# Loads, row products and stores in another order, and a batched routing over 54 pair sums, in a two-layer hybrid trunk

## The chip, the cores and the metric

The kernel runs on 1 core of one Trainium2 chip. The metric is the device time of a run in microseconds. Engines are named as in the profile: PE (TensorE matmul), PEld (its weight loads), DVE (VectorE), ACT (ScalarE), POOL (GpSimd) and SP (SyncE, which issues most DMAs).

## The reference

Two groups of tokens, 512 of `x_sample` and 128 of `x_prompt`, go through the same two layers, with other modulations. A layer is

```python
mod = jax.nn.silu(cond) @ p['ada_w'] + p['ada_b']
sh1, sc1, g1, sh2, sc2, g2 = jnp.split(mod[:, None, :], 6, axis=-1)
h = x * (1.0 + sc1) + sh1
mix, finals = _token_mix(h, p, lb, rot, s0)
x = _layernorm(ALPHA * x + g1 * mix, p['ln_g'][0], p['ln_b'][0])
h = x * (1.0 + sc2) + sh2
ffn = _peer(h, p['peer_wq'], p['peer_subkeys'], p['peer_u'], p['peer_v'])
x = _layernorm(ALPHA * x + g2 * ffn, p['ln_g'][1], p['ln_b'][1])
```

`_token_mix` runs three bidirectional scans (gated delta, retention, HGRN) and merges them. `_peer` is the expert stage, for blocks of 128 tokens, with 8 heads of 16 experts each out of 16384:

```python
s1, i1 = lax.top_k(s[:, :, 0], PEER_TOPK)
s2, i2 = lax.top_k(s[:, :, 1], PEER_TOPK)
cand_s = (s1[..., :, None] + s2[..., None, :]).reshape(PEER_BLOCK, R_HEADS, PEER_TOPK * PEER_TOPK)
cand_i = (i1[..., :, None] * N_KEYS + i2[..., None, :]).reshape(PEER_BLOCK, R_HEADS, PEER_TOPK * PEER_TOPK)
top_s, top_pos = lax.top_k(cand_s, PEER_TOPK)
idx = jnp.take_along_axis(cand_i, top_pos, axis=-1)
gate = jax.nn.softmax(top_s, axis=-1).astype(xb.dtype)
act = jax.nn.gelu(jnp.einsum('prkd,pd->prk', jnp.take(u_tab, idx, axis=0), xb))
return jnp.einsum('prk,prkd->pd', gate * act, jnp.take(v_tab, idx, axis=0))
```

Each token thus needs 128 rows of `peer_u` and 128 of `peer_v`, of 1024 float32 each. (The last two lines are drawn together here.)

## The kernel before

**Layout.** The 640 tokens are 5 blocks of 128, one token to a partition: blocks 0 to 2 are group B, 3 and 4 group A. Most buffers are views of one large `arena`; weights come in 2 MB `slab` loads, in an order that `slabs_of_layer` sets. SP runs one long list of DMA issues, and a wait in it holds up all that stands behind. Each engine's program is written out by hand, and `w(stage, name)` waits for a mark of another engine.

**A layer.** The modulation vectors are products of the condition with `ada_w` (`row_chunk`, L780, 512 columns each, their sums on DVE by `row_sum`, L1676) and go through DRAM (`mod_scratch`) to be spread over the partitions. Four of them are made at the very start, ahead of everything; the rest in the turns of the `hg` scan, two or three in a turn (`late_chunk`), each with a slab load of its own. `modulate` (L1680, L1682) makes `h`, PE transposes it (`to_features`, L791), the projections follow (L772, L831 for the small `wba`), then the three scans, then `merge`, `residual`, the queries (`peq`) of group A, and the experts.

**Experts.** The blocks come in the order 3, 4, 0, 1, 2, called e0 to e4 here. Each has a u phase and a v phase. In the u phase POOL issues 128 indirect gathers (L2367, one row for each token, 512 KB each) and DVE takes the dot of each with `h` (`dots`, L2213). In the v phase POOL gathers 128 rows of `peer_v`; PE adds 96 of them (`L1223`, four matmuls with a diagonal matrix made by ACT, L1589), DVE the other 32 (`sums`, L2241; each an axpy). Rows lie in a ring of slots: 8 for e0 and e1, 21 for e2 to e4. A gather can start only when its slot is free.

**Routing** is DVE work: for each head the top 16 of the two key sides (MAX8, FIND_INDEX8, MATCH_REPLACE8), 256 pair sums (L2106), their top 16, and the decode of the 16 winners into two key numbers (a comparison with `iota` L2131, a product L2134 and a sum L2137 over 256 elements for each side), 28 steps in all (`route_step`). Two heads of e0 are routed ahead of its dots and six among them, two steps for each dot; the routing of block e+1 lies in the v phase of e, three steps for each row that PE adds.

**What else lies among the dots.** In e0 u the merge of group B (one `merge_step` after every fifth dot, L2055 on DVE, behind PE's products), in e1 u the `finish` of e0 (11 operations) and the residual of group B (`residual("B")`, 12 operations for each of 3 blocks), in e2 to e4 the `finish` of the block before; one step after each dot. The residual writes the block's new x, which SP stores to `x_scratch` (`store_resid_block`, L494), then `hm` (L1724) and `h` (L1729). `h` goes to the place of the x that is being stored, so it waits for that store. On PE the list is: mixing of blocks 0 and 1, `to_features` of block 0, mixing of block 2 (L1166), `to_features` of block 1, and so on.

## Time and profile before

| | us |
|---|---|
| runs of the kernel | 6470.97, 6471.75, 6485.54; median 6471.75 |
| the profiled execution | 6502.23 |
| its span | 6500.40 |
| start, to the first projection | 109.6 |
| layer 0 to the first gathers | 1294.8 |
| experts of layer 0 | 1873.4 |
| between the layers, to the first projection | 57.8 |
| layer 1 to the first gathers | 1253.4 |
| experts of layer 1 | 1891.3 |
| end | 20.1 |

The shares of the span are: PE 73%, DVE 62%, POOL 47%, ACT 19%. They are averages over stages of two kinds. In the first 1300 us of a layer PE is nearly always busy and POOL hardly; in the experts POOL issues gathers all the time, and the DMA engines move 380 GB/s. So the profile is read stage by stage, and within the experts phase by phase.

### The profile page before, as it was taken

Reading aid. Unit: us, or ns where it says so; the run is one execution under the profiler, and the core shown is the slowest. Engines: PE = TensorE matmul, PEld = TensorE weight load, DVE = VectorE, ACT = ScalarE, POOL = GpSimd, SP = SyncE. Lnnn points to the kernel's source line nnn. Section 1 sums busy time; section 2 is a strip of 40 time slices with the busy share of each in tenths; the row PEclk is TensorE's granted clock in tenths of the full one; section 3 lists DMA queues with packets and bytes.
Section 4 is the critical chain, followed back from the end, with each engine's and each line's share of the span. In section 5 each row is a group of like instructions: output and inputs, shape, how many; then the busy total and the mean of one; then the engine's idle time right before and its main releaser. Section 6 shows DMA issues by size and latency. Waiting matters only on the chain. (4 is left out here: it accounts for less than half of the span.)

```text
span 6500.4 us, 53698 instructions
## 1 busy us (share of the span) xinstructions
PE 4738.0 (73%) x18289; PEld 2806.8 (43%) x18289; DVE 4029.9 (62%) x8153; ACT 1250.4 (19%) x2552; POOL 3075.3 (47%) x2828
## 2 busy tenths in 40 slices
PE   6999898998765718090979999889979564553628
PEld 3795644764323303040448946557534221221203
DVE  2561446159778696969235613661886887879682
ACT  1531142110211102020234312421011111110101
POOL 0000013027767777777700000220577677777775
PEclk8999999999887859595989999999989787776859
DMA  4001122469999999999920011125799899999997
GB/s 162 27 1 39 39 70 99 172 224 337 393 343 369 376 408 385 406 397 390 411 107 27 1 52 37 68 85 191 297 363 378 314 374 387 405 377 401 375 413 320
DMA packets 507384, 1628.23 MB, mean 250 GB/s; under 512 B 48336, under 2 KB 60774, under 8 KB 506934
## 3 DMA queue, kind: packets, MB, share of 16 engines
q0 software_dynamic: 368640, 1342.34, 53.4%
q1 hardware_dynamic: 138474, 282.46, 12.2%
q8 instruction: 149, 2.44, 0.2%
q14 instruction: 121, 0.99, 0.0%
HBM read 1605.65 MB, written 21.59 MB: 250 GB/s over the span
## 5 line engine op out<-in xcount | busy, mean ns | idle before, releaser
L1223 PE MATMUL ps<-slab,arena 128*128 128x512 f32 x896 | 402.7, 605 | 626.0 <-ACT arena L1589 623.2
L1223 PE MATMUL ps<-states,arena 128*128 128x512 f32 x1104 | 505.0, 606 | 216.5 <-ACT arena L1589 203.9
L1589 ACT ACTIVATE arena<-consts,arena 128x128 f32<-128x128 f32 x960 | 378.1, 401 | 1219.4 <-PE ps L1223 1215.1
L772 PE MATMUL ps<-hT,slab 128*128 128x512 f32 (+1 forms) x2048 | 566.0, 438 | 6.1 <-DVE arena L1751 6.1
L2367 POOL DMA_INDIRECT arena<-in_peer_u,peer_idxs x400 | 482.0, 1205 | 181.2 <-issue 98.2
L1223 PE MATMUL ps<-arena 128*128 128x512 f32 x1200 | 535.2, 594 | 13.5 <-DMA arena<-in_peer_v,peer_idxs 11.3
L1223 PEld LDWEIGHTS ps<-slab,arena 128*128 128x128 f32 x896 | 172.8, 194 | 849.6 <-issue 845.9
L2213 DVE CUSTOM_DVE_ANT_0 arena<-arena 128x1024 f32<-128x1024 f32 x400 | 494.9, 1245 | 35.7 <-DMA arena<-in_peer_u,peer_idxs 32.9
L1223 PE MATMUL ps<-hT,arena 128*128 128x512 f32 x544 | 245.4, 603 | 353.7 <-ACT arena L1589 353.0
L2322 POOL TENSOR_TENSOR slab<-slab,arena 128x256 f32<-128x256 f32 x140 | 163.8, 1194 | 689.3 <-ACT slab L1515 689.3
L2367 POOL DMA_INDIRECT states<-in_peer_u,peer_idxs x300 | 356.4, 1188 | 265.9 <-PE ps L1179 149.0
L2367 POOL DMA_INDIRECT arena<-in_peer_v,peer_idxs x400 | 415.4, 1038 | 124.7 <-issue 101.7
L1143 PE MATMUL ps<-hT,slab 128*128 128x256 f32 (+1 forms) x1536 | 436.3, 438 | 3.0 <-DVE arena L1751 3.0
L1223 PEld LDWEIGHTS ps<-states,arena 128*128 128x128 f32 x1104 | 211.2, 194 | 497.1 <-issue 484.7
L772 PEld LDWEIGHTS ps<-hT,slab 128*128 128x128 f32 x2048 | 313.9, 193 | 256.9 <-issue 256.9
L2294 POOL TENSOR_TENSOR arena<-arena,consts 128x512 f32<-128x512 f32 x20 | 25.8, 1310 | 831.1 <-DVE arena L1833 831.1
L2213 DVE CUSTOM_DVE_ANT_0 states<-states,arena 128x1024 f32<-128x1024 f32 x300 | 370.1, 1237 | 56.7 <-DMA states<-in_peer_u,peer_idxs 50.7
L2213 DVE CUSTOM_DVE_ANT_0 slab<-slab,arena 128x1024 f32<-128x1024 f32 x296 | 361.8, 1224 | 31.6 <-DMA slab<-in_peer_u,peer_idxs 20.6
L2367 POOL DMA_INDIRECT states<-in_peer_v,peer_idxs x300 | 312.5, 1042 | 113.2 <-issue 71.7
L1223 PEld LDWEIGHTS ps<-arena 128*128 128x128 f32 x1200 | 224.8, 190 | 310.7 <-issue 296.1
L2367 POOL DMA_INDIRECT slab<-in_peer_u,peer_idxs x296 | 312.8, 1057 | 90.2 <-issue 89.6
L1143 PEld LDWEIGHTS ps<-hT,slab 128*128 128x128 f32 x1536 | 296.9, 193 | 127.3 <-issue 6.1
(317 smaller groups left out, 8973.1 us busy)
## 6 DMA issues: line engine op xcount, KB each, us to landing
slab<-in_w_in SPq DMA_DIRECT2D x50, 2048.0 KB, 7.8
slab<-in_ada_w SPq DMA_DIRECT2D x24, 2048.0 KB, 8.3
arena<-in_w_branch SPq DMA_DIRECT2D x24, 1024.0 KB, 10.4
arena<-mod_scratch SPq DMA_DIRECT2D x36, 512.0 KB, 9.0
slab<-in_w_out SPq DMA_DIRECT2D x8, 2048.0 KB, 12.1
slab<-in_peer_wq SPq DMA_DIRECT2D x6, 2048.0 KB, 20.9
x_scratch<-arena SPq DMA_DIRECT2D x16, 512.0 KB, 5.7
arena<-in_peer_u,peer_idxs POOLq DMA_INDIRECT x400, 6.6
```

The source lines that it names most:

```text
L772: last = mm(bank(i0 + c, part), wt[:, k, c * P:(c + 1) * P], hT[:, k, t0:t0 + tn], start=(k == 0), stop=(k == KC - 1))
L1143: last = mm(ps[i % 2][:, 0:tn], slab_at(l, ("merge", g, m, hf))[:, k, c * P:(c + 1) * P], hT[:, k, t0:t0 + tn], start=(k == 0), stop=(k == ...
L1223: last = mm(ps[4 + half][:, :], diag[i % DIAGS], row(e, 1, j)[:, 512 * half:512 * half + 512], start=(i == 0), stop=(j == PE_SLOTS[-1]))
L1589: fn(diag[i % DIAGS], C["ident"], ACT.Copy, scale=PK["coef"][:, j:j + 1]).then_inc(diag_ready, 1)
L2213: v.tensor_tensor_reduce(out=row(e, 0, j), in0=row(e, 0, j), in1=h_block(e), scale=1.0, scalar=0.0, op0=ALU.mult, op1=ALU.add, accum_out=P ...
L2294: dn.pool.mark(g_.tensor_tensor(U["GRm"], U["GRm"], bc_mid(C[f"neg{d}"], H), ALU.add), ("GRm", d, n))
L2322: hg.pool.mark(g_.tensor_tensor(x, x, halves4(HG["k"][:, H * d:H * d + H, block_cols(n, d)], lv, d), ALU.mult), ("XK", lv, d, n))
L2367: g_.indirect_dma_start(out=row(e, table, j), out_offset=None, in_=rows_of, in_offset=bass.IndirectOffsetOnAxis(ap=PKU["idxs"][:, e * SLOT ...
```

## The change

**Routing.** A pair (i, j) of ranks can be among the best 16 sums only if (i+1)(j+1) is at most 16; the new routing forms 54 sums that hold all such pairs, in five rectangles. Heads are taken in batches: 2, then 3 and 3 in e0, 4 and 4 in the other blocks. The decode is done once a batch, with operations of 256 elements for each head in it (512, 768 or 1024). Among the dots of e0 three steps stand after each dot instead of two. `finish` begins at dot 4 (dot 6 in e1).

```diff
+RECTS = ((0, 0, 1, 16), (16, 1, 2, 8), (24, 2, 4, 5), (34, 4, 8, 3), (46, 8, 16, 1))
+N_CAND = 54
+BATCH = 4
...
+                def routing(e, first, last, spare):
+
+                    nr = last - first
...
+                            dve.wait_ge(scored, first + i + 1)
+                        for side in (0, 1):
+                            c, o = 256 * (first + i) + P * side, 32 * i + TOPK * side
+                            yield from top16(dk, tv[:, o:o + TOPK], ti[:, o:o + TOPK], PK["sc"][:, c:c + P], (i, side))
+                    w(dk, ("i1", (nr - 1, 1)))
+                    dk.mark(v.tensor_copy(tif, ti), "tif")
+                    yield
+
+                    tv3 = tv.rearrange("p (r k) -> p r k", k=2 * TOPK)
+                    cand3 = cand.rearrange("p (r c) -> p r c", c=N_CAND)
+                    for c0, i0, i1, n in RECTS:
+                        rows_, shape = i1 - i0, [P, nr, i1 - i0, n]
+                        dk.mark(tt(cand3[:, :, c0:c0 + rows_ * n].rearrange("p r (i j) -> p r i j", j=n),
+                                   tv3[:, :, i0:i1].unsqueeze(3).broadcast_to(shape),
+                                   tv3[:, :, TOPK:TOPK + n].unsqueeze(2).broadcast_to(shape), ALU.add), ("cand", c0))
+                        yield
+                    w(dk, ("cand", RECTS[-1][0]))
+                    for i in range(nr):
+                        o = TOPK * i
+                        yield from top16(dk, fv[:, o:o + TOPK], fp[:, o:o + TOPK], cand[:, N_CAND * i:N_CAND * (i + 1)], ("c", i))
+                    w(dk, ("i1", ("c", nr - 1)))
+                    dk.mark(v.tensor_copy(fpf, fp), "fpf")
+                    yield
+
...
+                    yield
+                    w(dk, "reached")
+                    dk.mark(tt(flat(spare), flat(reached), bc_mid(C["dstarts"], TOPK * nr), ALU.mult), "start_parts")
+                    yield
+                    w(dk, "start_parts")
+                    dk.mark(v.tensor_reduce(pj, flat(spare), AX.X, ALU.add), "start")
+                    yield
+                    w(dk, "d1")
+                    dk.mark(tt(four(reached), four(reached), tv3[:, :, 0:TOPK].unsqueeze(2).broadcast_to(shape), ALU.mult), "e1_parts")
+                    yield
+                    w(dk, "e1_parts")
+                    dk.mark(v.tensor_reduce(e1, flat(reached), AX.X, ALU.add), "e1")
+                    yield
+                    dk.mark(tt(pj, fpf, pj, ALU.subtract), "pj")
+                    yield
+                    w(dk, "pj")
+                    dk.mark(tt(flat(spare), bc_last(pj, TOPK), bc_mid(C["iota"], TOPK * nr), ALU.is_equal), "is_j")
+                    yield
+                    w(dk, "is_j")
+                    dk.mark(tt(four(spare), four(spare), ti3[:, :, TOPK:2 * TOPK].unsqueeze(2).broadcast_to(shape), ALU.mult), "e2_parts")
+                    yield
+                    w(dk, "e2_parts")
+                    dk.mark(v.tensor_reduce(e2, flat(spare), AX.X, ALU.add), "e2")
```

On DVE, in the order of its instructions in e0 u: ISA with 1024 elements is a dot, L2055 or L2088 a merge, L2131 to L2137 and L2169 to L2192 the decode. Before:

```order
L2131 TENSOR_TENSOR arena<-arena,consts 128x256
L2134 TENSOR_TENSOR arena<-arena 128x256
L2213 ISA arena<-arena 128x1024
L2213 ISA arena 128x1
L2137 TENSOR_REDUCE arena<-arena 128x16
L2131 TENSOR_TENSOR arena<-arena,consts 128x256
L2213 ISA arena<-arena 128x1024
L2213 ISA arena 128x1
L2055 TENSOR_TENSOR arena<-ps,arena 128x384
L2134 TENSOR_TENSOR arena<-arena 128x256
L2137 TENSOR_REDUCE arena<-arena 128x16
L2213 ISA states,arena<-states,arena 128x1024
```

The same place on DVE in e0 u, after:

```order
L2169 TENSOR_TENSOR arena<-arena,consts 128x768
L2172 TENSOR_REDUCE arena<-arena 128x48
L2175 TENSOR_TENSOR arena<-arena 128x768
L2262 ISA mod_row,arena<-mod_row,arena 128x1024
L2262 ISA arena 128x1
L2088 TENSOR_TENSOR arena<-ps,arena 128x384
L2178 TENSOR_REDUCE arena<-arena 128x48
L2180 TENSOR_TENSOR arena<-arena 128x48
L2183 TENSOR_TENSOR arena<-arena,consts 128x768
L2262 ISA arena<-arena 128x1024
L2262 ISA arena 128x1
L2186 TENSOR_TENSOR arena<-arena 128x768
```

One or two decode operations of 256 elements stood between two dots; now three steps, which are operations of 768 elements where they work on all winners of three heads.

```diff
-                for _ in routing(0, 0, 2):
+                for _ in routing(0, 0, 2, ACC_ALL[:, 0:512]):
...
-                dots(0, routing(0, 2, R_HEADS), lambda j: 2, (100, 122, 124, 126))
+
+                def rest_of_first_block():
+                    for first in (2, 5):
+                        yield from routing(0, first, first + 3, ACC_ALL[:, 0:768])
+                dots(0, rest_of_first_block(), lambda j: 3, (100, 122, 124, 126))
...
-                dots(1, finish_and_residual(), lambda j: 1, (0, 30, 32, 34))
+                dots(1, finish_and_residual(), lambda j: 1 if j >= 6 else 0, (0, 30, 32, 34))
...
-                    dots(e, finish(e - 1), lambda j: 1, (0, 30, 32, 34))
+                    dots(e, finish(e - 1), lambda j: 1 if j >= 4 else 0, (0, 30, 32, 34))
```

**Startup and layer start.** The third early slab goes to the buffer `a` at once; x is read straight into its place; the four sums are stored and reloaded ahead of the first projection slabs. PE waits for the small parameters (`params_loaded`) only after `to_features`, and for `wba` by a semaphore of its own. In layer 1, X and the modulations are loaded ahead of the small parameters.

```diff
+                load_slab(0, ("row", 2))
...
-            sp.dma_start(x_dram[0:NS], A["x_sample"].rearrange("a (b p) d -> (a b) p d", p=P)).then_inc(copied, 16)
-            sp.dma_start(x_dram[NS:NB], A["x_prompt"].rearrange("a (b p) d -> (a b) p d", p=P)).then_inc(copied, 16)
+            sp.dma_start(X[:, 0:NS, :], A["x_sample"].rearrange("a (b p) d -> p (a b) d", p=P)).then_inc(x_loaded, 16)
+            sp.dma_start(X[:, NS:NB, :], A["x_prompt"].rearrange("(b p) d -> p b d", p=P) if len(A["x_prompt"].shape) == 2
+                         else A["x_prompt"].rearrange("a (b p) d -> p (a b) d", p=P)).then_inc(x_loaded, 16)
...
                 names = slab_names[l]
                 setup.join(sp)
+                if l == 0:
+                    load_slab(0, ("row", 3))
+                else:
+                    sp.dma_start(X, x_dram.rearrange("b p d -> p b d")).then_inc(x_loaded, 16)
...
+                    load_mods_1()
                 sp.dma_start(rows[0:60, :], A["dn_conv_w"][bass.ds(l, 1)].rearrange("a k (b p) -> (a k b) p", p=P)).then_inc(params_loaded, 16)
                 sp.dma_start(rows[60:63, :], A["branch_norm_w"][bass.ds(l, 1)].rearrange("a n p -> (a n) p")).then_inc(params_loaded, 16)
...
-                sp.dma_start(wba[:, :, :], slab_src("in", l)[:, :, C_BA:C_BA + 16], allow_slow_non_contiguous=True).then_inc(params_loaded, 16)
+                sp.dma_start(wba[:, :, :], slab_src("in", l)[:, :, C_BA:C_BA + 16], allow_slow_non_contiguous=True).then_inc(wba_loaded, 16)
                 if l == 0:
-                    sp.wait_ge(copied, 32)
-                sp.dma_start(X, x_dram.rearrange("b p d -> p b d")).then_inc(x_loaded, 16)
-                if l > 0:
+                    sp.wait_ge(row_summed, EARLY)
+                    sp.dma_start(mod_dram[0, :, 0:EARLY * 512], EARLY_ROWS).then_inc(rows_stored, 16)
+                    sp.wait_ge(rows_stored, 16)
                     load_mods_1()
-                    load_slab(l, names[0])
-                    load_slab(l, names[1])
+                load_slab(l, ("dn", 0))
+                load_slab(l, ("dn", 1))
...
                 if l == 0:
-                    for name in names[2:first + 2]:
-                        load_slab(l, name)
-                    sp.wait_ge(row_summed, EARLY)
-                    sp.dma_start(mod_dram[0, :, 0:EARLY * 512], EARLY_ROWS).then_inc(rows_stored, 16)
-                    sp.wait_ge(rows_stored, 16)
-                    load_mods_1()
+                    sp.dma_start(x_dram[0:NS], A["x_sample"].rearrange("a (b p) d -> (a b) p d", p=P)).then_inc(copied, 16)
+                    sp.dma_start(x_dram[NS:NB], A["x_prompt"].rearrange("a (b p) d -> (a b) p d", p=P)).then_inc(copied, 16)
```

On SP, in the order of its issues, from the small loads to the reload of the modulations (`mod_scratch` is the DRAM copy of the modulations, `in_ada_w` a slab of the condition's products, `in_w_in` one of the projections). Before:

```order
L508 DMA small<-in_rt_log_decay 128x8
L510 DMA wba<-in_w_in 128x8x16
L513 DMA arena<-x_scratch 128x5x1024
L520 DMA states<-in_state_delta 128x4x128 x2
L520 DMA states<-in_state_ret 128x4x128 x2
L520 DMA states<-in_state_hgrn 128x4x128 x2
L434 DMA slab<-in_ada_w 128x8x512 x2
L434 DMA slab<-in_w_in 128x8x512 x2
L527 DMA mod_scratch<-arena 2x2048
L473 DMA arena<-mod_scratch 128x1024 x4
```

The same stretch of SP after, from the load of x on:

```order
L458 DMA arena<-in_x_prompt 128x1024
L440 DMA slab<-in_ada_w 128x8x512
L519 DMA rows<-in_dn_conv_w 60x128
L520 DMA rows<-in_branch_norm_w 3x128
L522 DMA small<-in_dn_a_log 128x8
L522 DMA small<-in_dn_dt_bias 128x8
L522 DMA small<-in_rt_log_decay 128x8
L524 DMA wba<-in_w_in 128x8x16
L527 DMA mod_scratch<-arena 2x2048
L481 DMA arena<-mod_scratch 128x1024 x4
L440 DMA slab<-in_w_in 128x8x512 x2
```

The store to `mod_scratch` and its reload stood behind the states and four slab loads; now they stand right behind the small loads, the fourth slab of `in_ada_w` ahead of those, and the third ahead of this stretch.

**Stores.** The block of an expert stage is stored once: to `x_scratch` in layer 0, to y in layer 1; MODE is loaded for three blocks of five.

```diff
+                if e < 3:
+                    load_mod(l, MODE, 5, 0 if b < NS else 1, mods_e_loaded)
...
-                sp.dma_start(x_dram[b], XE).then_inc(xe_stored, 16)
-                sp.dma_start(y, XE).then_inc(xe_stored, 16)
+                sp.dma_start(x_dram[b] if l < DEPTH - 1 else y, XE).then_inc(xe_stored, 16)
```

**Row products of the hg stage.** The second and third product of a turn stand after levels 2 and 4 (were 1 and 3) on PE, their sums after 4 and 6 (were 3 and 5) on DVE.

```diff
-                        if lv in (1, 3):
-                            late_chunk(n, 1 if lv == 1 else 2)
+                        if lv in (2, 4):
+                            late_chunk(n, lv // 2)
...
-                        if lv % 2 == 1 and lv // 2 < IN_TURN[l][n]:
-                            row_sum(l, chunk_no(l, n, lv // 2), ps[(3, 7, 3)[lv // 2]])
+                        for i, after in enumerate((1, 4, 6)):
+                            if lv == after and i < IN_TURN[l][n]:
+                                row_sum(l, chunk_no(l, n, i), ps[(3, 7, 3)[i]])
```

**Residual of group B.** `h` of a block comes after the layernorm of the next block, that of the last block four dots later.

```diff
+                def finish_h(i):
+
+                    b = BLOCKS[g][i]
+                    mods = MODR[g, 0 if b < NS else 1]
+                    h = HT[g][:, i, :]
+                    w(st.dve, ("hm", b))
+                    if g == "B":
+                        dve.wait_ge(xb_stored[i], 16)
+                    st.dve.mark(tt(h, h if g == "A" else HM, mods[:, 1, :], ALU.add), ("h", b))
...
+                        yield
                     hm = h if g == "A" else HM
+                    if i and g == "B":
+                        w(st.dve, ("h", b - 1))
                     st.dve.mark(tt(hm, xb, mods[:, 2, :], ALU.mult), ("hm", b))
                     yield
-                    w(st.dve, ("hm", b))
-                    if g == "B":
-                        dve.wait_ge(xb_stored, 16 * (i + 1))
-                    st.dve.mark(tt(h, hm, mods[:, 1, :], ALU.add), ("h", b))
+                    if g == "A":
+                        finish_h(i)
+                        yield
+                if g == "B":
+                    for _ in range(4):
+                        yield
+                    finish_h(len(BLOCKS[g]) - 1)
                     yield
```

On DVE in e1 u, around `h` of block 0 (L1729, then L1733; L1699 and L1713 are the last operation of a layernorm, L1724 and L1754 `hm`, L1716 and L1741 the first use of PE's mix, of block 1 before and of block 2 after; ISA with 1024 elements is a dot). Before:

```order
L1699 TENSOR_TENSOR arena<-arena 128x1024
L2213 ISA arena<-arena 128x1024
L2213 ISA arena 128x1
L1724 TENSOR_TENSOR arena<-arena 128x1024
L2213 ISA arena<-arena 128x1024
L2213 ISA arena 128x1
L1729 TENSOR_TENSOR arena<-arena 128x1024
L2213 ISA arena<-arena 128x1024
L2213 ISA arena 128x1
L1716 TENSOR_TENSOR arena<-ps,arena 128x512
```

On DVE in e1 u around L1733, after:

```order
L1713 TENSOR_TENSOR arena<-arena 128x1024
L2262 ISA arena<-arena 128x1024
L2262 ISA arena 128x1
L1733 TENSOR_TENSOR arena<-arena 128x1024
L2262 ISA arena<-arena 128x1024
L2262 ISA arena 128x1
L1754 TENSOR_TENSOR arena<-arena 128x1024
L2262 ISA states,arena<-states,arena 128x1024
L2262 ISA arena 128x1
L1741 TENSOR_TENSOR arena<-ps,arena 128x512
```

L1729 stood ahead of the next block's L1716; L1733 of block 0 now stands behind the layernorm of block 1 (L1713), one dot, L1754 and another dot ahead of L1741, which reads the mix of block 2. PE's own list is the same in this place.

## Rows read from the trace of the kernel before

**Rows 1.** windows, experts: length; PE, PEld, DVE, ACT, POOL; clock, DMA, GB/s
```profile
1404.40:3277.80 1873.40, 1153.43 (x2810) 541.91 (x2810) 1424.97 (x3100) 253.44 (x585) 1395.73 (x1296) 0.81 0.98 380
```

**Rows 2.** windows of L2367 by phase: length, POOL busy (count), clock, DMA, GB/s
```profile
1414.00:1656.00 242.00, 155.40 (x127) 0.92 0.96 356
1839.00:2062.00 223.00, 159.53 (x128) 0.71 0.91 335
2234.00:2409.00 175.00, 136.25 (x128) 0.52 1.00 393
2745.40:2915.10 169.70, 130.66 (x129) 0.96 1.02 398
3091.40:3255.20 163.80, 124.79 (x128) 0.96 1.03 411
```

**Rows 3.** timeline of a v phase: start us, us, engine, line, operation
```profile
2416.97 0.43 DVE L2134 TENSOR_TENSOR arena<-arena 128x256 f32<-128x256 f32 x1
...
2417.03 1.18 POOL L2367 DMA_INDIRECT states<-in_peer_v,peer_idxs  x1 [0.30 <-issue]
...
2419.89 0.94 POOL L2367 DMA_INDIRECT arena<-in_peer_v,peer_idxs  x1 [0.30 <-issue]
...
2420.97 1.28 DVE L2241 SCALAR_TENSOR_TENSOR arena<-states,arena 128x1024 f32<-128x1024 f32 x1 [1.06 <-DMA states<-in_peer_v,peer_idxs]
2421.14 1.93 POOL L2367 DMA_INDIRECT arena<-in_peer_v,peer_idxs  x1 [0.30 <-issue]
```

**Rows 4.** timeline of the startup: SP's issues and PE's row products
```profile
23.12 0.35 SPq L505 DMA_DIRECT2D rows<-in_dn_conv_w  x1
...
29.42 15.61 PE L780 MATMUL ps<-slab,small 128*2 128x512 f32 x32
...
46.87 13.90 PE L780 MATMUL ps<-slab,small 128*2 128x512 f32 x32 [1.84 <-DMA slab<-in_ada_w]
...
61.58 0.26 SPq L527 DMA_DIRECT2D mod_scratch<-arena  x1
68.71 1.76 SPq L473 DMA_DIRECT2D arena<-mod_scratch  x4
...
77.82 1.23 DVE L1680 TENSOR_TENSOR arena<-arena 128x1024 f32<-128x1024 f32 x1 [16.27 <-DMA arena<-mod_scratch]
```

**Rows 5.** timeline of the hg stage of layer 1, in one turn
```profile
4188.36 0.23 SPq L463 DMA_DIRECT2D mod_scratch<-mod_row  x1
...
4190.20 0.23 SPq L456 DMA_DIRECT2D mod_row<-in_ada_b  x1
...
4190.37 8.69 PE L780 MATMUL ps<-slab,small 128*2 128x512 f32 x16 [4.19 <-DMA slab<-in_ada_w]
```

**Rows 6.** timeline of the boundary between the layers
```profile
3291.06 0.58 SPq L513 DMA_DIRECT2D arena<-x_scratch  x1
...
3306.06 1.23 DVE L1680 TENSOR_TENSOR arena<-arena 128x1024 f32<-128x1024 f32 x1 [11.04 <-DMA arena<-mod_scratch]
```

**Rows 7.** windows of e0 u, parted where its routing ends; columns as above
```profile
1412.00:1581.00 169.00, 151.01 (x446) 86.39 (x445) 164.16 (x428) 11.10 (x21) 113.51 (x95) 0.96 0.96 358
1581.00:1657.00 76.00, 41.80 (x128) 23.57 (x126) 58.77 (x97) 6.93 (x12) 62.56 (x50) 0.82 0.96 354
```

**Rows 8.** DVE by line, e3 v and first dots after: busy, mean ns
```profile
L2213 DVE CUSTOM_DVE_ANT_0 slab<-slab,arena 128x1024 f32<-128x1024 f32 x6 | 7.4, 1226 | 0.3
L2134 DVE TENSOR_TENSOR arena<-arena 128x256 f32<-128x256 f32 x16 | 6.8, 424 | 0.5
```

**Rows 9.** DVE by line in e0 u, until its routing ends
```profile
L2055 DVE TENSOR_TENSOR arena<-ps,arena 128x384 f32<-128x384 f32 x17 | 9.4, 551 | 0.0
```

**Rows 10.** waits of DVE in e1 u (total, times, longest); two timeline rows
```profile
DVE arena L1729 <- DMA x_scratch<-arena: 13.8, 3, 9.3
...
1883.45 1.23 DVE L1729 TENSOR_TENSOR arena<-arena 128x1024 f32<-128x1024 f32 x1 [2.56 <-DMA x_scratch<-arena]
...
1886.49 15.60 PE L1166 MATMUL ps<-slab,arena 128*128 128x512 f32 x32
```

211 lines of the change are left out of this document (96 added, 115 removed).

## The prediction

> **What bounds the kernel now.** I read the busy time by stage first [rows 1]. The expert stage takes 1873.4 us of a layer with the DMA share at 0.98, POOL busy for 1395.7 of it and PE for 1153 and DVE for 1425. So a routing with fewer DVE operations does not by itself shorten an expert phase: it does so only where DVE is late or holds up POOL. Next I read POOL's gathers phase by phase [rows 2]. A gather that nothing disturbs takes POOL 0.94 us, and 0.30 of issue lies between two of them, so 128 of them need at least 159 us. The last v phase, which has no routing in it, takes 163.8; one with routing takes 169.7 (e3). There the whole of what routing costs is some 6 us. The two u phases with extra DVE work are the long ones: e0 u 242, e1 u 223.
>
> What makes a gather longer than 0.94 is read from single rows [rows 3]. One that starts inside a 256-element TENSOR_TENSOR (2416.97, 0.43 long) takes 1.18 and ends 0.81 after that operation's end; one that starts inside a 1024-element SCALAR_TENSOR_TENSOR (2420.97, 1.28 long) takes 1.93 and ends 0.82 after it. The row between, with no such operation at its start, is at 0.94. Gathers that begin during MAX8, FIND_INDEX8, MATCH_REPLACE8 or TENSOR_REDUCE are also at 0.94 in the gathers I went through. So DVE work with two inputs is what POOL pays for, and how long one such operation lasts matters, not only how many there are.
>
> The Trainium skill has a rule for this: its page "GPSIMD Engine Reference", in the table of key figures at its start, says that GpSimd's SBUF interfaces are shared with VectorE, and that DVE instructions with two SBUF inputs contend with it. By that rule the change works against itself: its decode puts operations with two inputs together into longer ones. The trace agrees on which operations count [rows 3]; the page has no price, and the sum goes by the rows.
>
> **The change part by part** (the profiled execution took 6502.23 us, 30.5 above the median of 6471.75; the terms are differences and I subtract them from the median).
>
> *Startup.* Now [rows 4] the setup is over by 23.12, when the first small load goes out behind it; the row products wait for those loads, start at 29.42, run 15.61, wait 1.84 for the third slab and run 13.90 more, to 60.8. The sums are stored at 61.58, but their reload goes out only at 68.71, since the store stands behind slab loads in the queues, and the first modulate is at 77.82. After: the third slab goes out ahead of the masks that the setup waits for, 2.1 MB that at the 390 GB/s of the expert phases [rows 2] are 5.4 us: setup over at about 28.5. PE doesn't wait for the small loads any more and starts then. No wait for the third slab is left: the products end near 57.9, 3 earlier. The store then goes through empty queues; such a store takes 1.84 from its issue to the next one behind it (4188.36 to 4190.20 [rows 5]), not 7.1, so 5 more. Rows and exponentials that ran before are now in the way for under 1. I take -8, between -3 (the store as slow as now) and -12 (the reload itself faster). The slabs of the first projection go out after the reload; 30 us of modulate and transposes cover them.
>
> *Boundary and end.* At the layer's end two stores of the last block are waited for; then X goes out behind six small loads of some 0.4 each, at 3291.06, the modulations behind it, and modulate starts at 3306.06 [rows 6]. With X and the modulations first, X goes out 2.5 earlier, and with one store less the wait before is up to 2 shorter: -4 (-2 to -6). At the end of the program one of the two stores falls away: -1.5 (0 to -3).
>
> *Products of the hg stage.* At 4190.37 PE stood 4.19 for a slab [rows 5]. A later product would remove this wait, but the level's own masking on DVE reached only to about then, so what is gained is near 0.6 for each of 9 turns: -5, between 0 and 9 products of 2.05 off the path, -18.
>
> *Routing in e0 u.* DVE is the bound while it routes: 84 dots in the 169 us from 1412, 2.01 each, with DVE busy for 164.2; then 43 in 76 us, 1.76 each [rows 7]. A dot with its read-out is some 1.3 [rows 8] and every fifth brings a merge of 0.55 [rows 9], 118.6 in all, which leaves 7.6 for each of six heads. A head now gives up 256 sums for 54 in five steps (0.42 to perhaps 0.2: 1.1 less), and its decode goes from six operations of 256 elements at 0.42 [rows 8] and six small ones to a third of eight of 768 (between 0.42 for 256 elements and 1.23 for 1024 [rows 4, 8], near 0.95 each: 2.5) and of the small ones (0.9 less). That makes 5.6, so 12 for the six. But the change also takes three steps a dot where two were, so the routing stands in the first 44 dots: 44 x 1.3 + 9 x 0.55 + 6 x 5.6 = 96, with the idle share of now 99. The next 41 dots are no longer DVE's: PE is busy for 151.0 of the 169 with the merges of group B, about 7.5 every fifth dot, and nothing in the tail runs under 1.4 a dot: 1.4 to 1.76, 57 to 72, I take 66. The last 43 stay at 76. That gives 241 against the 169 + 76: **-4** for each layer, -8 (each between -13 and, if the new head costs what the old did, +8). Most of the gain goes into DVE time in which PE or POOL is the bound.
>
> *Residual B in e1 u.* DVE waits 13.8 us in three pieces for the stores of the residual blocks, because `h` is written over what a store reads and the dots queue behind it [rows 10]. With `h` of a block behind the next block's layernorm, some 15 us later, the first two of these waits go. But PE has `to_features` of block 0 (ready when `h` is) queued ahead of the mixing of block 2, 15.60 us that started at 1886.49, right behind `h` at 1883.45 [rows 10]. Between the new `h` and the first half of that mix DVE has one modulate and two dots, about 3.6 us; PE has 2 of transposes and 8 of mixing. DVE then stands about 6.4, and about 4.2 for the second half, with the dots queued behind. The query slabs, which wait for that mix, go out later too, and the store of block 2 behind them, so that its wait keeps about 5. Removed 13.8, put in its place 15.6: +2 a layer, +4 (each -10 if mix b2 is done in time, +10 if the ring of 8 slots runs dry as well).
>
> *v phases.* A block has 40 two-input operations of 256 elements now (a head's sums, two comparisons and two products), 0.42 each [rows 8]. A gather that starts inside one ends 0.81 after it, so it only grows if more than 0.13 of the operation is left (0.94 less 0.81). One of 0.42 meets a start in 0.42 / 1.245 of the cases and then costs 0.10 on average: 1.35 a block. After there are 10 of 1024 elements, near 1.2 each, which meet a start nearly every time and cost 0.6 + 0.81 - 0.94 = 0.47: 4.7. Routing ends at axpy 18 of 32 instead of 24, since it has fewer steps, and an axpy with routing around it costs its gather 0.3 more than one without: -1.8. Of the 1.6 left I take half, +0.8, because in e0 and e1 PE is busy for most of the v phase and a later gather is partly hidden by it: eight phases, **+6**. Ends: -2 each if the long operations fall between gathers, +5 each if every one meets a gather at full length.
>
> *Finish, mods and the rest.* `finish` from dot 4 or 6 instead of 0, three MODE loads instead of five, and the double gate buffer move nothing that is waited for, and the two heads that are routed ahead of the first gather end before PE's queries, which it waits for: 0; the cover is the rest of the u phase and the v phase, before the block's buffer is needed again.
>
> *Sum:* -8 - 4 - 1.5 - 5 - 8 + 4 + 6 = -16.5; from 6471.75 that is **6455**.
>
> **The rivals.** (A) *The routing's gain comes through.* If the 41 dots run at 1.4 and the last 43 too, as in e2 u (175 for 128 gathers [rows 2]), e0 u is 26 shorter a layer: -16.5 + 8 - 52 = -60, 6411; with half of it, 6433. For it: nothing in the dots themselves needs 1.76. Against it: those dots run at 1.76 in this trace although DVE doesn't route any more [rows 7]. (B) *Long two-input operations lock POOL, slower.* In a burst of the decode each gather takes up to 1.97 and is issued every 2.28 instead of 1.245. At five such in each half of a block, +5 a phase, 40 in all instead of 6, and with e0 u at its +8: -16.5 - 6 + 40 + 24 = +41, 6513; with e0 u as forecast 6489. The point from which it decides is some nine of ten long operations with a gather at full length. The Trainium skill ("GPSIMD Engine Reference", the row on the SBUF interfaces) leads here; [rows 3] bear it out for single gathers, and [rows 2] speak against its size, since all that routing costs a v phase today is 6 us. (C) *The ring in e1 u runs dry* on the new wait for PE, +10 a layer, the rest as forecast: 6471, no change. (D) *The startup does nothing*, since the masks' delay eats the earlier store: 6463, no change.
>
> **How the numbers follow.** A measurement of this kernel can tell about 0.3% from no change: 6452 and 6491 are the marks. My forecast has 0.48, own range 6440 to 6470; 0.18 of it is below the lower mark and 0.30 within. A has 0.26, faster. C 0.07 and D 0.05 are within, B 0.14 slower. Faster 0.44, same 0.42, slower 0.14. The range takes in A but for its extreme, and B at its lower end: 6418 to 6494; 2 in 10 lie beyond.
>
> **What would show it.** In the profile after: first modulate near 70 instead of 77.8; first load of layer 1 to modulate shorter by 2 to 3; in e1 u no wait for stores on the first two blocks, and in its place one for PE's mix, 6 and 4 us long; e0 u between 232 and 253, with the first 44 dots in 99 us; gathers in v phases near 1.9 in bursts where the 1024-element operations stand, and a phase with routing 168 to 175 long. I am wrong if e0 u falls below 230 (A), if a v phase passes 175 (B; e0 v, 183 now, aside), or if PE has the mix of block 2 done when DVE comes for it.

## The result: slower by a third of a per cent

The changed kernel takes 6495.88 us (median of 20 runs, 6471.4 to 6528.85), the kernel before 6477.73 (20 runs, 6460.17 to 6490.99): a ratio of 1.0034, 95% interval 1.0023 to 1.0045. Its profiled execution has a span of 6501.1, next to 6500.4 before, which is longer than any of its 20 runs. So the two traces are compared by stretches, and the runs by their medians.

Ahead of the experts the change does what was forecast, or more. The startup after, as in [rows 4]:

```profile
29.13 15.36 PE L793 MATMUL ps<-slab,small 128*2 128x512 f32 x32 [21.25 <-DVE small L1678]
...
59.04 0.26 SPq L527 DMA_DIRECT2D mod_scratch<-arena  x1
60.74 1.75 SPq L481 DMA_DIRECT2D arena<-mod_scratch  x4
...
70.30 1.23 DVE L1694 TENSOR_TENSOR arena<-arena 128x1024 f32<-128x1024 f32 x1 [11.30 <-DMA arena<-mod_scratch]
```

The reload follows the store after 1.7 us instead of 7.1, and modulate starts 7.5 earlier. The first gather of layer 0 starts at 1378.9 instead of 1404.5; from the last axpy of layer 0 to the first gather of layer 1 it is 1312.9 instead of 1327.2. With the end that is 43 us. The experts give it back: 1881.9 and 1894.9 instead of 1857.3 and 1876.2, from the first gather to the last axpy. Both traces are single executions: i_before_1store (below), whose code is that of before up to this point, has its first gather at 1399.3, 5 earlier than before.

Within the experts, u phases are longer and some v phases shorter. Of e0 u (two stretches, columns as in [rows 7]):

```profile
1386.00:1490.00 104.00, 82.11 (x246) 46.78 (x245) 100.75 (x286) 6.20 (x11) 62.89 (x52) 0.97 0.90 324
1490.00:1640.00 150.00, 109.61 (x328) 63.26 (x328) 113.49 (x184) 11.82 (x21) 124.85 (x94) 0.88 0.97 358
```

DVE is full in the first stretch, where all of the routing now is, and idle for a quarter of the second. The phase takes 253.9 (first dot to last) where it took 244.8.

The gathers of e2 u, e3 u and e4 u, in both layers (columns as in [rows 2]):

```profile
2219.30:2409.50 190.20, 151.18 (x129) 0.52 0.97 361
2578.10:2752.10 174.00, 135.30 (x128) 0.52 1.00 392
2918.40:3096.00 177.60, 138.60 (x129) 0.52 1.00 383
5426.10:5602.60 176.50, 137.50 (x129) 0.53 1.00 388
5769.50:5947.70 178.20, 139.51 (x128) 0.52 0.99 379
6114.10:6302.00 187.90, 149.19 (x128) 0.52 0.97 360
```

Before, e3 u of layer 0 and e4 u of layer 1 in the same view:

```profile
2577.00:2753.00 176.00, 136.74 (x129) 0.52 1.00 393
6125.70:6301.00 175.30, 136.20 (x129) 0.51 1.01 395
```

All six took 175.6 to 176.2 before (first dot to last). Two are now 12 to 14 longer, with POOL busier by as much for the same 128 gathers, and the DMA share at 0.97 instead of 1.00.

### The profile page after: what moved, and what is told of

The parts are those of the page before. It is cut to its first block and busy times, and to the rows that moved or that the text cites. A ratio compares the mean times of both kernels' runs of the same rounds, so it can differ in the third digit from the quotient of the medians.

```text
span 6501.1 us, 52845 instructions
## 1 busy us (share of the span) xinstructions
PE 4723.5 (73%) x18289; PEld 2814.4 (43%) x18289; DVE 3828.2 (59%) x7335; ACT 1249.8 (19%) x2552; POOL 3107.2 (48%) x2828
## 5 line engine op out<-in xcount | busy, mean ns | idle before, releaser
L2420 POOL DMA_INDIRECT arena<-in_peer_u,peer_idxs x400 | 497.2, 1243 | 151.2 <-issue 104.9
L2420 POOL DMA_INDIRECT states<-in_peer_u,peer_idxs x300 | 378.9, 1263 | 288.9 <-PE ps L1193 150.7
L2420 POOL DMA_INDIRECT slab<-in_peer_u,peer_idxs x296 | 334.6, 1130 | 90.2 <-issue 90.2
```

Of the source, the lines that this page charges most:

```text
L2420: g_.indirect_dma_start(out=row(e, table, j), out_offset=None, in_=rows_of, in_offset=bass.IndirectOffsetOnAxis(ap=PKU["idxs"][:, e * SLOT ...
```

## What a short and a long u phase look like

In the timeline of e3 u after, a short one, POOL's gathers and DVE's dots run in step:

```profile
2660.16 0.97 POOL L2420 DMA_INDIRECT slab<-in_peer_u,peer_idxs  x1 [0.31 <-issue]
...
2660.37 1.23 DVE L2262 CUSTOM_DVE_ANT_0 arena<-arena 128x1024 f32<-128x1024 f32 x1
2661.44 0.96 POOL L2420 DMA_INDIRECT slab<-in_peer_u,peer_idxs  x1 [0.30 <-issue]
...
2661.66 1.23 DVE L2262 CUSTOM_DVE_ANT_0 arena<-arena 128x1024 f32<-128x1024 f32 x1
```

A gather starts 0.16 before the end of a dot and ends 0.81 after it, so it takes 0.96, and both engines advance by 1.28. In e2 u after, a long one:

```profile
2328.03 1.23 DVE L2262 CUSTOM_DVE_ANT_0 hT<-hT,arena 128x1024 f32<-128x1024 f32 x1 [0.39 <-DMA hT<-in_peer_u,peer_idxs]
2328.75 1.32 POOL L2420 DMA_INDIRECT states<-in_peer_u,peer_idxs  x1 [0.30 <-issue]
...
2331.51 1.23 DVE L2262 CUSTOM_DVE_ANT_0 hT<-hT,arena 128x1024 f32<-128x1024 f32 x1 [0.69 <-DMA hT<-in_peer_u,peer_idxs]
2331.92 1.62 POOL L2420 DMA_INDIRECT states<-in_peer_u,peer_idxs  x1 [0.30 <-issue]
```

A row lands late, its dot starts late, the next gather starts in the middle of that dot and takes 1.3 to 1.6 instead of 0.96; so its row lands late too, and the delay comes back some five dots later. I call lead the number of gathers begun when dot j starts, less j. It is 6 to 7 from dot 40 on in all six phases of before, and 5 in the two long ones of after.

## The experts: which part of the change does it

The times are medians; e0 u and the six u phases of e2 to e4 are from the profile of each kernel (layer 0; layer 1). A profile is one execution, and some are far from the median: that of a_front is its slowest run (6526), as is that of q_start (6497, next section), that of o_route its fastest (6447). Each kernel was compared with before in runs taken beside it, and the median of before went from 6476 to 6481 over these; after was run once, so a difference from after is a few us less certain than the intervals say. e1 u is left out: with the code of after it takes anything from 210 to 234 in these profiles, with other stores or without.

| kernel | us | ratio to before, interval | e0 u | e2 to e4 u |
|---|---|---|---|---|
| a_front | 6487 | 0.9992 to 1.0023 | 249; 247 | 177, 183, 183; 190, 191, 182 |
| b_finish0 | 6492 | 1.0006 to 1.0038 | 254; 254 | 180, 187, 177; 176, 178, 176 |
| c_e0spread | 6480 | 0.9988 to 1.0019 | 245; 248 | 190, 175, 189; 179, 180, 197 |
| d_resid | 6490 | 1.0010 to 1.0044 | 255; 257 | 176, 187, 182; 176, 181, 178 |
| f_stores | 6462 | 0.9966 to 0.9989 | 254; 253 | 177, 176, 176; 177, 177, 178 |
| g_pad | 6535 | 1.0071 to 1.0113 | 255; 258 | 188, 186, 182; 193, 179, 186 |
| h_spread_pad | 6529 | 1.0059 to 1.0097 | 245; 249 | 190, 183, 193; 200, 182, 187 |
| i_before_1store | 6509 | 1.0026 to 1.0065 | 245; 246 | 176, 186, 175; 176, 178, 189 |
| j_mode | 6463 | 0.9958 to 0.9985 | 253; 254 | 179, 176, 177; 177, 176, 184 |
| k_2store | 6465 | 0.9960 to 0.9992 | 252; 253 | 177, 193, 176; 178, 174, 176 |
| p_late | 6487 | 1.0005 to 1.0025 | 255; 256 | 180, 181, 180; 185, 183, 178 |

**First four.** My theory was that the new order inside the experts makes the loss: routing packed into 44 dots, the later `finish`, the later `h`.

> The change without its expert part: startup, layer start, stores and row products of the hg stage as after; routing, dots, finish and residual B as before. In the two profiles all ahead of the experts is 43 us shorter after and the experts 44 longer. Theory 1 (the loss is made by the new order inside the experts): about 6440, 0.994 of before, e0 u near 245 and all u phases of e2 to e4 at 175 to 177. Rival (the earlier stages hand the experts over in another state, or their gain is given back by DMA traffic): 6465 or more, with u phases of 185 to 190 among e2 to e4.

The routing, dots and `finish` calls and the residual's order of before were put back. The rival came true: hardly faster than before, with five of six u phases long, though the expert code differs from before only in its stores and MODE loads. So the long phases don't need the new routing. (That it has five may owe something to its profile being its slowest run.)

> After, with finish among the dots from dot 0 again (e1 to e4). Theory 1a (the later start of finish leaves DVE without a row in hand when the phase settles, so e2 to e4 fall out of the 1.27 us rhythm): u phases of e2 to e4 all at 175 to 178, 20 to 30 us less than after, about 6470. Rival (the state comes from how the v phase ahead ends, or by chance): some u phases at 185 to 190 still, 6490 to 6500.

```diff
-                    dots(e, finish(e - 1), lambda j: 1 if j >= 4 else 0, (0, 30, 32, 34))
+                    dots(e, finish(e - 1), lambda j: 1, (0, 30, 32, 34))
```

Within 4 us of after, and a phase at 187: the start of `finish` is not it.

> After, with e0's routing among its dots thinner once the first batch is through: three steps a dot up to dot 22, then one and two in turn. Theory 1b (e0 u is longer since routing packed in 44 dots leaves a tail that POOL bounds at 1.8 us a dot): e0 u goes from 254 to 245 or below, 15 to 20 us less in all, about 6478. Rival (e0 u is longer for the long two-input operations themselves, wherever they stand): e0 u stays at 250 to 255, 6490 to 6500.

```diff
-                dots(0, rest_of_first_block(), lambda j: 3, (100, 122, 124, 126))
+                dots(0, rest_of_first_block(), lambda j: 3 if j < 22 else 1 + j % 2, (100, 122, 124, 126))
```

As theory 1b has it: e0 u is back at 245 and 248, and the whole 16 below after, although three of the six u phases are long.

> After, with h of a residual block of group B right behind its hm again, as before. In the profile after the waits for stores (13.8 us) are gone and waits for PE's mix of block 2 stand there instead (10.9). Theory (one wait for the other): within 6 us of after, 6490 to 6502, e1 u 222 to 234. Rival (the delayed h costs through the later query slabs and PE): 8 us or more below after, 6488 or less.

```diff
-                    if i and g == "B":
-                        finish_h(i - 1)
-                        yield
...
-                    if g == "A":
-                        finish_h(i)
-                        yield
+                    finish_h(i)
+                    yield
...
```

5 below after, where the interval is some 11 wide to either side: one wait for the other, as expected, and no more than that can be told.

**The stores.** What a_front shares with after in the experts is one store less for a block and two MODE loads less in a layer. In before, in e2 u, it can be seen what these do:

```profile
2260.84 0.32 SPq L479 DMA_DIRECT2D arena<-x_scratch  x1
2261.20 0.43 SPq L473 DMA_DIRECT2D arena<-mod_scratch  x1
...
2266.87 1.22 DVE L2213 CUSTOM_DVE_ANT_0 arena<-arena 128x1024 f32<-128x1024 f32 x1 [2.06 <-DMA arena<-in_peer_u,peer_idxs]
...
2269.81 1.23 DVE L2213 CUSTOM_DVE_ANT_0 slab<-slab,arena 128x1024 f32<-128x1024 f32 x1 [1.70 <-DMA slab<-in_peer_u,peer_idxs]
```

Two loads of 512 KB go out among the rows, XE (L479, the block's x) and MODE (L473, its modulation). Some 4 us later DVE stops for a row for 2.06 and then for 1.70, POOL goes on issuing, and the lead goes from 4 at dot 16 to 6 or 7. That was theory 2.

> After, with both stores of an expert block and MODE loaded for all five blocks again, as before. In a_front, whose experts have the code of before but for one store and two MODE loads less, e2 to e4 u are at 177 to 191 instead of 176. Theory 2 (lead): in before the two loads of 512 KB hold up rows in flight at about dot 18, DVE stands some 5 us, POOL goes on, and from then on 6 or 7 rows are ahead of DVE; this puts every gather's start near the end of a dot (1.27 a dot). With fewer transfers the lead stays at 5 and the rhythm breaks. Then here: lead 6 or 7 from dot 40 on, e2 to e4 u all at 175 to 178, 20 to 35 us less than after: 6460 to 6475. Rival (the slow u phases come from elsewhere in the change or by chance): u phases of 183 to 190 still, 6488 to 6500.

```diff
-                sp.dma_start(x_dram[b] if l < DEPTH - 1 else y, XE).then_inc(xe_stored, 16)
+                sp.dma_start(x_dram[b], XE).then_inc(xe_stored, 16)
+                sp.dma_start(y, XE).then_inc(xe_stored, 16)
```

(and MODE without its condition; the counts that are waited for follow). 34 below after, and all six phases short, lead 6 to 8 from dot 40 on. Three of them in the windows of POOL's gathers, columns as in [rows 2]:

```profile
2209.00:2386.30 177.30, 137.69 (x131) 0.53 1.00 391
2551.40:2727.00 175.60, 136.59 (x129) 0.54 1.01 393
...
6076.50:6254.50 178.00, 138.68 (x130) 0.52 1.00 389
```

> Before, with only the stores and MODE loads of the change (one store of an expert block, MODE for three blocks). Theory 2 (lead): 7 MB of traffic less, yet slower: lead 5 in some u phases of e2 to e4, which take 180 to 191, and 15 to 40 us longer than before: 6490 to 6515. Rival: the same as before or a few us faster, 6470 to 6481, u phases at 176.

The opposite edit, in before: 0.46% slower with less to transfer, and two phases long. Both and a short one, in the same view:

```profile
2565.00:2751.00 186.00, 146.99 (x129) 0.52 0.98 365
2924.40:3099.60 175.20, 135.89 (x130) 0.51 1.00 392
...
6117.00:6306.10 189.10, 150.09 (x129) 0.51 0.97 359
```

Both directions agree. That part of the change alone costs more (31 and 34 us) than the change loses as a whole (18).

> After, with MODE loaded for all five blocks again, and one store of a block. f_stores (both stores and all MODE loads) had lead 6 to 8 and e2 to e4 u at 176 to 178 in all six, at 6462. Theory 2a (what counts is what holds up rows in flight at dots 16 to 25, that is XE and MODE together): e3 and e4 u back at 175 to 178, 6465 to 6475. Theory 2b (the second store counts): no change from after, 6488 to 6500, e3 and e4 u above 180 in about half.

> After, with both stores of an expert block again, and MODE for three blocks. Theory 2a (XE and MODE together count): no change from after, 6488 to 6500, e3 and e4 u above 180 in about half, e2 u at 176. Theory 2b (the second store counts): e2 to e4 u at 175 to 178, 6462 to 6472.

Either one is enough, 33 and 31 below after; neither of my two forms was right in excluding the other. One long phase each is left, so both together are safer. Over all the profiles the count is clear: in the eight kernels with both stores and all MODE loads (before, f_stores and the six of the next section) one of 48 such phases is over 180 us; in the six with neither, and without the MAX8 that follows, 17 of 36 are.

**How a transfer that nobody waits for helps.** I first read the lead as rows that lie ready for DVE.

> After, with one more DVE operation after dot 40 of e2 to e4: a MAX8 over 1024 elements, whose result nothing reads. Theory 2 (lead): a stop of DVE alone of some 1.2 us lets POOL gain a row; lead 6 or 7 afterwards, e2 to e4 u at 177 to 180 in spite of the added work, and the whole 10 to 25 us shorter than after, 6470 to 6485. Rival (the DMA traffic itself, not the lead): as after or 7 us longer, 6496 to 6503, u phases of 185 to 192.

```diff
+                        if e >= 2 and j == 40:
+                            v.max(PK["tv"][:, 0:8], h_block(e))
```

39 above after. But the run doesn't decide what the lead is, since the MAX8 didn't raise it: in the four phases that had a lead of 6 at dot 40 it fell to 3 or 4 by dot 50 (the other two had 5 already). From e2 u of layer 0, which was in step until then:

```profile
2280.22 0.97 POOL L2423 DMA_INDIRECT slab<-in_peer_u,peer_idxs  x1 [0.30 <-issue]
...
2281.57 1.22 DVE L2266 MAX8 arena<-arena 128x8 f32<-128x1024 f32 x1
2282.72 1.21 DVE L2262 CUSTOM_DVE_ANT_0 arena<-arena 128x1024 f32<-128x1024 f32 x1
2282.76 1.97 POOL L2423 DMA_INDIRECT slab<-in_peer_u,peer_idxs  x1 [0.31 <-issue]
...
2284.99 1.22 DVE L2262 CUSTOM_DVE_ANT_0 slab<-slab,arena 128x1024 f32<-128x1024 f32 x1
2285.04 1.99 POOL L2423 DMA_INDIRECT slab<-in_peer_u,peer_idxs  x1 [0.30 <-issue]
...
2291.27 1.23 DVE L2262 CUSTOM_DVE_ANT_0 slab<-slab,arena 128x1024 f32<-128x1024 f32 x1 [0.46 <-DMA slab<-in_peer_u,peer_idxs]
```

The MAX8 moves the dots against the gathers. The next gather starts 0.04 after the start of a dot and takes 1.97. The dots follow each other every 1.14, so two of them pass to one gather, and the next three gathers start in the same place again (1.99 each). For four gathers POOL issues one every 2.28, DVE uses up the rows that it had, and from 2291.27 on it waits.

> After, with both the thinner routing in e0 u of c_e0spread and the one MAX8 of g_pad. c_e0spread had e0 u at 245 and 248 and still 190, 189 and 197 among e2 to e4 u, at 6480. Theory 2 (lead): e2 to e4 u at 177 to 180, so 15 to 25 us below c_e0spread: 6455 to 6465, under before by about 20. Rival: 6480 as c_e0spread, or longer by the 7 us of added work.

The same: 6529, 48 above c_e0spread. A stop of DVE alone takes gathers away, so these two runs can't tell rows that lie ready for DVE from rows that are still on the way. My second reading was that what helps are rows on the way, held up in the DMA queues. The test moves the MODE load to dot 64:

> After, with MODE loaded for all five blocks, but in e2 to e4 only when dot 64 is done (j_mode loads it at about dot 18, 6463). Theory 2c (rows in flight held up at any time put the phase right): where the first 64 dots run slow, the last 60 run at 1.27 to 1.3 a dot and the lead grows by one at dot 64; 6465 to 6485. Rival (only the start of the phase counts): the lead stays at 5 where it is 5 at dot 40, u phases of 183 to 192 in half of the six, 6488 or more.

```diff
+                    if e >= 2:
+                        sp.wait_ge(dot_done, SLOTS * e + 64)
                     load_mod(l, MODE, 5, 0 if b < NS else 1, mods_e_loaded)
```

In each of the six phases the lead is higher by one at dot 80 than at dot 56 (by two in one), where the two long phases of after stay at 5 from dot 40 to 110; and the four that had a lead of 5 at dot 40 take 21.9 to 23.2 us for 16 dots between dots 32 and 64, 20.5 to 21.4 between 80 and 112. Two of them, e3 u of both layers, ahead of the load and behind it (POOL's gathers, columns as in [rows 2]):

```profile
2609.00:2662.40 53.40, 41.51 (x40) 0.50 0.99 376
2684.10:2737.00 52.90, 40.66 (x41) 0.50 1.03 409
5813.30:5867.00 53.70, 42.12 (x39) 0.50 0.99 368
5890.70:5943.60 52.90, 40.40 (x42) 0.50 1.03 411
```

The DMA engines move 409 and 411 GB/s instead of 376 and 368. So the load helps at dot 64 too, as theory 2c has it. (The lead can also rise by itself: from 5 to 6 ahead of the load in the first of these two, and in e3 u of layer 1 of after.) The whole, 6487, is 2 above the bound that I had set, since the first half of these phases still runs slow. That what counts is the rows waiting in the DMA queues, and not something else that a load does, is argued from the DMA share, not shown by itself.

## The parts ahead of the experts, and a faster version

> f_stores (after with both stores and all MODE loads again) with the row products of the hg stage after levels 1 and 3, as before. By the two profiles the products moved saved 16 us in layer 0 and 9 in layer 1: then here 6462 + 24 = about 6486. By the prediction's term they saved 5: 6467.

```diff
-                        if lv in (2, 4):
-                            late_chunk(n, lv // 2)
+                        if lv in (1, 3):
+                            late_chunk(n, 1 if lv == 1 else 2)
```

(and their sums on DVE after 3 and 5). 6485.78, 23.5 above f_stores.

> Before with only the row products of the hg stage after levels 2 and 4. If the moved products give what n_hg showed (23) also with the old experts: 6456. If the experts give it back: 6470 to 6480, with the first gather 16 us earlier all the same and the expert stages longer by as much.

6466.72, 0.9964 to 0.9992 of before: 14 less, between 5 and 23.

> f_stores with routing, finish and residual B as before, so before with the startup, the layer start and the hg products of the change. By the profiles the front is worth some 40 us and the batched routing costs 9 in each e0 u and gives back 20 in the v phases: 6481 - 40 = 6441 here, and u phases of e2 to e4 at 175 to 178. If the routing of the change is a gain in itself: above 6462. If the front alone makes the u phases slow also with these stores: 6465 or more, with u phases above 182.

6465.5 (0.9970 to 0.9993), 3 from f_stores: routing, `finish` and residual together change nothing that this can tell. But it is only 13 below before, where 37 were due. The 37 stand on two single traces, the one of before longer than all its runs; by runs alone the parts of the front give 14 (r_hg) and 2 (q_start, next), which agrees with 13.

> Before with only the startup and the layer start of the change (both stores, all MODE loads, routing, residual and hg products as before). If these give the 13 us that the profiles show (7 at the start, 6 between the layers) and the experts are as before: 6466. If o_route's missing 24 us are lost by them (experts longer behind another start): 6485 or more.

6478.4 (0.9986 to 1.0012), 2 below before. Its own profile has the first gather 13.7 us earlier than before and the stretch between the layers 5 shorter, and one u phase at 188. Whether the experts give these back or the interval (9 us below to 8 above) hides a part stays open: that profile is its slowest run.

> f_stores with the thinner routing in e0 u of c_e0spread. Both causes added: e0 u from 253 to 245, e2 to e4 u at 176 to 178, so 14 to 18 less than f_stores: about 6446, 0.995 of before. Rival (the two overlap): 6462 as f_stores.

6445.53, 0.9925 to 0.9966: the two causes add.

> l_spread_stores, and PE makes to_features of the three residual blocks of group B behind all three mixings, not between them. The wait for PE's mix of block 2 (10.9 us in e1 u after, 7.6 and 3.3) goes. Theory 3 (that wait took the place of the one for the stores): e1 u 8 to 10 shorter, 16 to 20 less than l_spread_stores: about 6430. Rival (POOL with 8 slots bounds e1 u anyway, or the later to_features delays the queries of group B): within 6 of l_spread_stores.

```diff
-                        if i:
+                        if i and g == "A":
                             to_features(st, b - 1, before, HT[g][:, i - 1, :])
                             before = b - 1
+                    if g == "B":
+                        for i, b in enumerate(BLOCKS[g][:-1]):
+                            to_features(st, b, before, HT[g][:, i, :])
+                            before = b
```

6423.91, **0.9887 to 0.9933 of before**: 22 less again, the fastest of all. DVE no longer waits for PE's mix in e1 u, which takes 200 and 211 (223 and 220 in l_spread_stores; but 212 and 210 in c_e0spread, with that wait, so the gain is shown by the runs and not by this phase alone).

## Why the prediction was wrong

The forecast was 6455, with faster at 0.44; the run gave 6496, just above the range of 6418 to 6494. As a difference it was -16.5, and +18 was measured; the 6471.75 that it started from, a median of three runs, was 6 low.

*The step that failed* is "`finish`, mods and the rest: 0". I looked for who waits for the MODE loads and the second store, found nobody, and wrote nothing. That nothing waits for them doesn't make them free to take out: without them the change is 34 us slower than with them (f_stores), since with them the u phases of e2 to e4 stay in step. The prediction uses the 175 of e2 u in [rows 2] only as a rate that e0 u could reach (rival A), and doesn't ask what keeps the phase there. With 34 taken off, the change stands at 6462, in the forecast's own range of 6440 to 6470, and 13 below the before of its runs. That this is near -16.5 is luck: e0 u lost 27 more than forecast, the products gained 9 to 18 more and the v phases 18 more, and these errors nearly cancel.

*Startup* -8: 7.5 in the profile. *Boundary* -4: from the store of the last block to modulate 24.5 instead of 28.3, -3.8. *End* -1.5: -2.7.

*Products of the hg stage* -5: 14 (r_hg) to 23.5 (n_hg), around my far bound of 18. This term was mis-sized. I took one turn's wait, 4.19, and let DVE's work that ends at the same time stand for all turns. By line, in layer 0, before and then after:

```profile
L780 PE MATMUL ps<-slab,small 128*2 128x512 f32 x192 | 100.6, 685 | 35.0 <-DMA slab<-in_ada_w 31.4 <-DVE states L1767 3.6
L1103 PE MATMUL ps<-slab 128*128 128x128 f32 x560 | 68.6, 278 | 1.2 <-DVE slab L2012 1.2
L1090 PE MATMUL ps<-arena 128*128 128x128 f32 x80 | 10.9, 281 | 8.1 <-DVE states L1767 6.7 <-ACT arena L1502 1.5
```

```profile
L793 PE MATMUL ps<-slab,small 128*2 128x512 f32 x192 | 91.2, 631 | 12.3 <-DMA slab<-in_ada_w 6.8 <-DVE states L1800 5.5
L1117 PE MATMUL ps<-slab 128*128 128x128 f32 x560 | 73.0, 292 | 20.5 <-DVE slab L2044 20.4
L1104 PE MATMUL ps<-arena 128*128 128x128 f32 x80 | 10.9, 281 | 2.1 <-ACT arena L1516 1.5 <-DVE states L1800 0.3
```

The wait for slabs fell by 24.6, a wait for DVE ahead of the levels' products (L1103, then L1117) rose by 19, one ahead of L1090 (then L1104) fell by 6, and the row products themselves took 9.4 less. Together these lines are 14 us shorter, and so is the stage: from the first L1070 to the last L1111 it took 274.7, from the first L1084 to the last L1125 after 261.1; in layer 1 238.9, then 230.0. r_hg has 263.1 and 229.4 there, so in the stage itself the moved products are worth 21 to 23 us.

*e0 u* -4 a layer: +9.1 and +9.4. The first stretch was nearly right: 44 dots took 101.7 (forecast 99). The tail was mis-sized: 84 dots in 152, 1.81 each, where I took 142, 1.69 each. I had said that the gain would go where POOL or PE is the bound; it went further, below zero. c_e0spread shows that the packing does it: with the same operations spread thinner e0 u is back at 245 and 248.

*Residual B*: the new wait is there, near the size forecast (7.6 and 3.3, where 6.4 and 4.2 were forecast). DVE's waits in e1 u of layer 0 after (total, times, longest):

```profile
DVE arena L1741 <- PE ps L1180: 10.9, 2, 7.6
```

The third store's wait is gone, which I had kept at 5. That it is a bound of e1 u is shown by m_all, and d_resid shows no difference between old and new order beyond its interval of some 11.

*v phases* +0.8 each: from the last dot to the last axpy e2 v and e3 v are 166 to 169 instead of 168 to 174, e1 v 1 to 5 longer; the eight together are 12 shorter, where +6 was forecast. e1 v takes 177.0 and 175.3, past the 175 that the prediction had set as the sign of rival B, but it took 172.2 and 174.5 before, and the other phases went the other way. The mechanism of rival B failed at its decisive point. From e3 v after:

```profile
2790.02 1.27 DVE L2166 TENSOR_TENSOR arena<-arena,consts 128x1024 f32<-128x1024 f32 x1
2790.03 0.94 POOL L2420 DMA_INDIRECT arena<-in_peer_v,peer_idxs  x1 [0.30 <-issue]
2791.27 0.94 POOL L2420 DMA_INDIRECT slab<-in_peer_v,peer_idxs  x1 [0.30 <-issue]
2791.32 1.23 DVE L2169 TENSOR_TENSOR arena<-arena,consts 128x1024 f32<-128x1024 f32 x1
...
2793.72 1.21 DVE L2175 TENSOR_TENSOR arena<-arena 128x1024 f32<-128x1024 f32 x1
2793.77 1.98 POOL L2420 DMA_INDIRECT slab<-in_peer_v,peer_idxs  x1 [0.30 <-issue]
```

A gather that starts just ahead of the long operation, or with it, is not held (0.94). One that starts 0.05 after it is, at 1.98. Since these operations take 1.22 and follow each other at nearly POOL's own 1.245, a batch costs one such hit in e2 v and e3 v, not five. I had averaged over starts as if they were independent. What these phases gained lies in the axpys: before, 6 to 11 gathers of such a phase took over 1.5, nearly all of them started inside an axpy; after it is 3 to 5 in all, the one hit of each batch included. Why fewer meet an axpy isn't shown. What the prediction called a burst, a gather every 2.28, did come, but in a u phase and behind a MAX8 (g_pad).

That operations with two inputs are what POOL pays for is also not the whole of it: in before the 14 gathers that start inside the layernorm's TENSOR_SCALAR of 1024 elements (L1693, one such input) and well ahead of its end take 1.27 on the median and end 0.81 after it, and those that start inside the additions that read one input from PSUM (L2055, L1716) stay at 0.94.

## What to carry to other kernels

Where two engines and the DMA queues advance at nearly the same pace, the pace is a state, and a part of the kernel that nobody waits for can hold it: before a "useless" transfer is taken out, look whether it delays something that then runs more evenly. A u phase that takes 176 us six times out of six needs an explanation as much as one that varies. And an average over random starts is no price for an operation whose length is near the period of what it meets.

## What was not expected of the hardware

Taking transfers out made the kernel slower by 0.26 to 0.65% (i_before_1store). In the u phases of after with a lead of 5 the DMA engines were busy 0.97 of the time and moved 360 GB/s, in those with 6 0.99 to 1.00 and 379 to 392; POOL was busy 13 to 14 us longer for the same 128 gathers in the two long ones than before. One added DVE operation of 1.22 in each of six phases cost 39 us, more than five times its own length: where a gather starts 0.04 after a dot and two dots pass to a gather, it meets a dot in the same place each time.
